# Row tiles for transposes and rotated scores, and a block transpose on DVE for a scan's input

## What is computed

```
# even layer: the scan's input, per group 512 + 128 + 128 channels
xbc = jax.nn.silu(causal_depthwise_conv(ssd_xbc, ssd_conv_w) + ssd_conv_b)
...
y_b = y_b.reshape(b_, l_, SSD_WIDTH) * jax.nn.silu(ssd_z.astype(jnp.float32))
# first block: 8 + 8 heads of 128, scores, softmax (or stick breaking), times v
z = jnp.einsum('bqhd,bkhd->bhqk', q[:, t0:t1], kb).astype(jnp.float32) * scale
# odd layer: 16 latent heads, 128 nope and 64 rotated channels
q_full = jnp.concatenate([q_nope, q_rope], axis=-1)
k_full = jnp.concatenate([k_nope, k_rope], axis=-1)
y_c = causal_block_attention(q_full, k_full, v) * jax.nn.silu(z_c)
```

## Time and profile before

| | |
|---|---|
| median of 3 runs (lowest, highest) | 2646.15 us (2645.53, 2647.1) |
| the profiled execution, its time | 2647.85 us |
| the profiled execution, its span | 2646.3 us |
| granted TensorE clock, mean | 0.999 |
| busy: PE / PE weight load / DVE / ACT / POOL | 2628.7 / 2181.9 / 1560.7 / 1346.5 / 337.9 us |

### The profile page before, as it was taken

The page is one execution under the profiler, slowest core; times in us unless marked ns, Lnnn a source line. Parts: engine busy times, 40 slices in busy tenths (PEclk is TensorE's granted clock), DMA queues, the critical chain, the costliest instruction groups (busy, mean ns, idle before and its releaser), DMA issues. The chain is left out here.

```text
span 2646.3 us, 35764 instructions
## 1 busy us (share of the span) xinstructions
PE 2628.7 (99%) x12125; PEld 2181.9 (82%) x12125; DVE 1560.7 (59%) x1825; ACT 1346.5 (51%) x1784; POOL 337.9 (13%) x523
## 2 busy tenths in 40 slices
PE   9999999999999999999999999999999999999998
PEld 7888888888878888888888888888888889888887
DVE  6444456667555555555555664445877855556864
ACT  6544455655444444444444654446665545554443
POOL 2100032211100000000000111000110010123400
PEclk9999999999999999999999999999999999999999
DMA  8966686678866767666666787666777777777864
GB/s 308 311 230 216 219 234 220 208 247 268 246 214 211 226 210 227 208 226 224 219 218 207 262 254 238 204 211 228 239 235 231 247 248 227 235 260 218 219 234 160
DMA packets 175722, 611.79 MB, mean 231 GB/s; under 512 B 23185, under 2 KB 26305, under 8 KB 175361
## 3 DMA queue, kind: packets, MB, share of 16 engines
q1 hardware_dynamic: 133632, 485.03, 55.4%
q0 software_dynamic: 37184, 121.07, 15.5%
q10 hardware_dynamic: 4800, 4.26, 0.6%
HBM read 559.36 MB, written 52.47 MB: 231 GB/s over the span
## 5 line engine op out<-in xcount | busy, mean ns | idle before, releaser
L1872 DVE TENSOR_TENSOR w_lo<-raw,w_hi 128x1024 fp32r<-128x1024 f32 x918 | 1115.4, 1222 | 850.9 <-ACT w_hi L1284 843.9
L1284 ACT ACTIVATE w_hi<-raw 128x1024 fp32r<-128x1024 f32 x919 | 963.8, 1058 | 901.0 <-PE acc L830 780.9
L824 PE MATMUL acc<-w_hi,x_t_hi 128*128 128x512 f32 (+1 forms) x2400 | 950.8, 396 | 0.4 <-ACT w_hi L1284 0.4
L824 PE MATMUL acc<-w_hi,x_t_lo 128*128 128x512 f32 (+1 forms) x2400 | 933.8, 389 | 0.0
L830 PE MATMUL acc<-w_lo,x_t_hi 128*128 128x512 f32 (+1 forms) x2400 | 640.0, 388 | 2.7 <-DVE w_lo L1872 2.7
L830 PEld LDWEIGHTS acc<-w_lo,x_t_hi 128*128 128x128 f32 x2400 | 450.5, 188 | 95.6 <-DVE w_lo L1872 3.1
L824 PEld LDWEIGHTS acc<-w_hi,x_t_hi 128*128 128x128 f32 x2400 | 451.4, 188 | 91.9 <-issue 1.9
L824 PEld LDWEIGHTS acc<-w_hi,x_t_lo 128*128 128x128 f32 x2400 | 451.4, 188 | 91.0 <-issue 1.9
L824 PE MATMUL acc<-w_hi,ff_t_hi 128*128 128x512 f32 x352 | 136.9, 389 | 0.0
L824 PE MATMUL acc<-w_hi,ff_t_lo 128*128 128x512 f32 x352 | 136.9, 389 | 0.0
L830 PE MATMUL acc<-w_lo,ff_t_hi 128*128 128x512 f32 x352 | 94.1, 389 | 0.0
(11 more groups left out here) (394 smaller groups left out, 2654.8 us busy)
## 6 DMA issues: line engine op xcount, KB each, us to landing
raw<-stream SPq DMA_DIRECT2D x919, 512.0 KB, 4.3
d_in<-tile POOLq DMA_DIRECT2D x20, 512.0 KB, 3.6
d_ev<-tile POOLq DMA_DIRECT2D x20, 512.0 KB, 4.9
d_x<-tile POOLq DMA_DIRECT2D x16, 512.0 KB, 4.2
r_b<-d_x POOLq DMA_DIRECT2D x64, 128.0 KB, 6.2
xin<-d_x POOLq DMA_DIRECT2D x16, 512.0 KB, 7.5
d_h<-tile POOLq DMA_DIRECT2D x14, 512.0 KB, 4.8
h_b<-d_h POOLq DMA_DIRECT2D x56, 128.0 KB, 4.5
```

What stands on the lines that cost most here:

```text
L824: nc.tensor.matmul(out, src[x][:, chunk + c, t * P:(t + 1) * P], w_hi[:, s, w], start=first and c == 0 and x == 0, stop=False)
L1284: nc.scalar.activation(w_hi[:, u.slot, :], raw[:, u.slot, :], ACT.Copy).then_inc(hi_ready, 1)
L1872: nc.vector.tensor_tensor(w_lo[:, s, :], raw[:, s, :], w_hi[:, s, :].bitcast(F32), ALU.subtract).then_inc(lo_ready, 1)
```

## The change

1. Scan: the 12 transposes of u are one block transpose on DVE (`turn_u`, after four loads of 32-partition blocks instead of three), with the weight's columns grouped for it; silu is ACT's own function instead of tanh and a product; the jobs of p = 9 to 14 move one unit later.
2. `turn_rows`: a transpose of 128 rows is written as two of 64 rows, at tile positions (0, 0) and (64, 0), into two banks. It takes the place of L1096 (8 blocks), L908 and L1234 (3 blocks each). The copies behind it are two instead of one. At L1234 the second bank is `ps_y[:, TOK:]`, with a wait on `l_y` at q = 3.
3. Latent scores: those of both heads of a pair stand at the even head's unit, nope in full matmuls, the rotated part as two row tiles of 64 rows, the heads in two banks, `ps_s` and `turn[0]`.
4. The loop of attention's four passes is written out on TensorE.

```
 HEAD_AT_UNIT = (1, 3, 6, 9)
+
+
+def rows_of(ap, h):
+    return ap.rearrange("p (b h n) -> p b h n", h=2, n=HALF)[:, :, h, :]
...
         def load_u(g):
-            pool.dma_start(u_in[:, :, 0:512], ev_v[:, :, bass.ds(g.times(512, 1024), 512)]).then_inc(s_u, 16)
-            for m in range(2):
-                pool.dma_start(u_in[:, :, 512 + m * P:640 + m * P],
-                               ev_v[:, :, bass.ds(g.times(P, 3072 + 512 * m), P)]).then_inc(s_u, 16)
+            for b in range(P // SQ):
+                w = 1024 + 768 * g.k + 6 * SQ * b
+                pool.dma_start(u_b[b * SQ:(b + 1) * SQ, :, :],
+                               d_ev[:, w:w + 6 * SQ].rearrange("(a j) n -> j a n", j=SQ)).then_inc(s_u, 16)
...
+        def turn_rows(blocks, banks=turn):
+
+            for n, src in enumerate(blocks):
+                for h in range(2):
+                    r = slice(HALF * h, HALF * (h + 1))
+                    mm = nc.tensor.transpose(banks[h][:, HALF * n:HALF * (n + 1)], src[r, :], ident[r, r],
+                                             tile_position=(HALF * h, 0))
+            return mm
+
         def turn_tile(n, src, ready, value):
 
             pe.wait_ge(ready, value)
@@ -904,10 +920,7 @@
                 if p == HEAD_AT_UNIT[j] + 5:
                     pe.wait_ge(at_prob[kind], m.times(1, 1))
                     pe.wait_ge(at_pt, J.times(1, 1))
-                    for c in range(3):
-                        mm = nc.tensor.transpose(turn[1][:, c * P:(c + 1) * P],
-                                                 prob[kind][:, c * P:(c + 1) * P], ident[:, :])
-                    mm.then_inc(at_pt_ps, 1)
+                    turn_rows([prob[kind][:, c * P:(c + 1) * P] for c in range(3)]).then_inc(at_pt_ps, 1)
...
-        with pe.Fori(0, 4) as i:
+        for i in range(4):
             for b in range(2):
                 pe.wait_ge(sums_out, blk("win", 12 + b, i).times(1, 1))
-            if p == 0:
-                pe.wait_ge(s_u, n.times(48, 48))
+            if p == 7:
                 pe.wait_ge(dt_v, 7)
                 pe.wait_ge(s_yb, n.times(1, 1))
-                for c in range(6):
-                    bank = (turn[0], turn[1], ps_s)[c // 2]
-                    for t in range(TH):
-                        mm = nc.tensor.transpose(bank[:, (c % 2 * TH + t) * P:(c % 2 * TH + t + 1) * P],
-                                                 u_in[:, t, c * P:(c + 1) * P], ident[:, :])
-                mm.then_inc(s_ut, 1)
-            if p == 7:
                 pe.wait_ge(s_silu, n.times(1, 1))
-                for t in range(TH):
-                    for c in range(4):
-                        mm = nc.tensor.transpose(turn[t][:, c * P:(c + 1) * P], cv[:, c, t * P:(t + 1) * P],
-                                                 ident[:, :])
-                mm.then_inc(s_xt, 1)
+                turn_rows([cv[:, c, t * P:(t + 1) * P] for t in range(TH) for c in range(4)]).then_inc(s_xt, 1)
                 nc.tensor.transpose(ps_s[:, 0:P], cv[:, 4, 0:P], ident[:, :])
                 for t in range(TH):
                     w = slice(t * P, (t + 1) * P)
                     mm = nc.tensor.matmul(ps_s[:, (1 + t) * P:(2 + t) * P], cv[:, 4, w], cv[:, 5, w],
                                           start=True, stop=True)
                 mm.then_inc(s_cb, 1)
-            if p == 9:
+            if p == 10:
                 pe.wait_ge(s_xde, n.times(1, 1))
                 nc.tensor.matmul(ps_s[:, :], bm_t[:, :], xde[:, :], start=True, stop=True).then_inc(s_st, 1)
-            if p == 11:
+            if p == 12:
                 pe.wait_ge(s_m, n.times(1, 1))
                 pe.wait_ge(s_xd, n.times(1, 1))
...
                     pe.wait_ge(l_qk, J // 2 + 1)
                     pe.wait_ge(l_qr, J // 2 + 1)
                     pe.wait_ge(l_z, J + 1)
-                    q_n, k_n, q_r = lqk[:, s, 0, :], lqk[:, s, 1, :], lr[J // 2 % 2]
-                    for out, qw, kw in ((ps_s[:, 0:P], slice(0, P), slice(0, P)),
-                                        (ps_s[:, P:H3], slice(P, TOK), slice(0, TOK))):
-                        nc.tensor.matmul(out, q_n[:, qw], k_n[:, kw], start=True, stop=False)
-                        mm = nc.tensor.matmul(out, q_r[:, qw], kr_t[:, s, kw], start=False, stop=True)
-                    mm.then_inc(l_scores, 1)
+                    q_r = lr[J // 2 % 2]
+                    parts = ((slice(0, P), slice(0, P), slice(0, P)), (slice(P, H3), slice(P, TOK), slice(0, TOK)))
+                    for at, qw, kw in parts:
+                        for e, bank in enumerate((ps_s, turn[0])):
+                            nc.tensor.matmul(bank[:, at], lqk[:, e, 0, qw], lqk[:, e, 1, kw], start=True, stop=False)
+                        for e, bank in enumerate((ps_s, turn[0])):
+                            r = slice(HALF * e, HALF * (e + 1))
+                            mm = nc.tensor.matmul(bank[:, at], q_r[r, qw], kr_t[r, e, kw], start=False, stop=True,
+                                                  tile_position=(HALF * e, 0))
+                    mm.then_inc(l_scores, 2)
                 if q == 3:
                     pe.wait_ge(l_exp, J + 1)
                     pe.wait_ge(l_qr, min((J + 1) // 2 + 1, 8))
-                    for c in range(3):
-                        mm = nc.tensor.transpose(turn[1][:, c * P:(c + 1) * P], lp[s][:, c * P:(c + 1) * P],
-                                                 ident[:, :])
-                    mm.then_inc(l_pt_ps, 1)
+                    pe.wait_ge(l_y, J + 1)
+                    turn_rows([lp[s][:, c * P:(c + 1) * P] for c in range(3)], (turn[1][:, :], ps_y[:, TOK:]))\
+                        .then_inc(l_pt_ps, 1)
                 if q == 4:
                     pe.wait_ge(l_pt, J + 3)
...
+            if p == 1 and g:
+                decays(n, 1)
             if p == 3 and g:
                 open_decays(n)
             if p == 4:
                 act.wait_ge(s_conv, n.times(3, 3))
-                nc.scalar.activation(th[:, :], cv[:, :, :].rearrange("p c t -> p (c t)"), ACT.Tanh)\
-                    .then_inc(s_th, 1)
-            if p == 5:
+                c_ = cv[:, :, :].rearrange("p c t -> p (c t)")
+                nc.scalar.activation(c_, c_, ACT.Silu, scale=2.0).then_inc(s_silu, 1)
                 act.wait_ge(s_z, n.times(16, 16))
-                nc.scalar.activation(zth[:, :, :], zt[:, :, :], ACT.Tanh, scale=0.5).then_inc(s_zth, 1)
+                nc.scalar.activation(zt[:, :, :], zt[:, :, :], ACT.Silu).then_inc(s_zs, 1)
             if p == 7:
                 act.wait_ge(s_xt, n.times(1, 1))
-                for t in range(TH):
-                    last = nc.scalar.activation(xs[:, t, :], turn[t][:, :], ACT.Copy)
+                for h in range(2):
+                    last = nc.scalar.activation(rows_of(xs[:, :, :].rearrange("p t n -> p (t n)"), h), turn[h][:, :],
+                                                ACT.Copy)
                 last.then_inc(s_xs, 1)
-            if p == 9:
+            if p == 10:
                 act.wait_ge(s_st, n.times(1, 1))
                 nc.scalar.activation(st[:, :], ps_s[:, :], ACT.Copy).then_inc(s_state, 1)
-            if p == 12:
+            if p == 13:
                 act.wait_ge(s_yg, n.times(1, 1))
                 for t in range(TH):
                     last = nc.scalar.activation(zth[:, t, :], yb[:, t, :], ACT.Square,
                                                 accum_out=g_ss[:, t:t + 1])
...
                     dve.wait_ge(at_pt_ps, J.times(1, 1))
-                    nc.vector.tensor_copy(p_t[s][:, :], turn[1][:, 0:H3]).then_inc(at_pt, 1)
+                    for h in range(2):
+                        last = nc.vector.tensor_copy(rows_of(p_t[s][:, :], h), turn[h][:, 0:H3 // 2])
+                    last.then_inc(at_pt, 1)
...
+        def turn_u(g):
+
+            dve.wait_ge(s_u, 64 * (g + 1))
+            dve.wait_ge(s_conv, 3 * g)
+            nc.vector.transpose(u_t[:, :, :].rearrange("p c (a i) -> p c a i", i=SQ),
+                                u_b[:, :, :].rearrange("p a (c i) -> p c a i", i=SQ)).then_inc(s_ut, 1)
...
-            if p == 5:
-                dve.wait_ge(s_th, n.times(1, 1))
-                c_ = cv[:, :, :].rearrange("p c t -> p (c t)")
-                nc.vector.scalar_tensor_tensor(out=c_, in0=th[:, :], scalar=1.0, in1=c_,
-                                               op0=ALU.add, op1=ALU.mult).then_inc(s_silu, 1)
-            if p == 6:
-                dve.wait_ge(s_zth, n.times(1, 1))
-                nc.vector.scalar_tensor_tensor(out=zt[:, :, :], in0=zth[:, :, :], scalar=1.0, in1=zt[:, :, :],
-                                               op0=ALU.add, op1=ALU.mult).then_inc(s_zs, 1)
...
+            if p == 10:
                 for t in range(TH):
                     x_ = xs[:, t, :].rearrange("p (h d) -> p h d", h=HG)
```

(50 more changed lines are left out.)

1 line of the change is left out of this document (removed).

## The result

| | before | changed |
|---|---|---|
| median (lowest, highest), 4 runs each | 2645.92 us (2645.53, 2647.1) | 2661.38 us (2658.57, 2664.95) |
| the profiled execution's span | 2646.3 us | 2660.8 us |
| granted TensorE clock, mean | 0.999 | 0.997 |

What follows compares the result with a forecast made beforehand. TensorE, busy 99% of the span, was taken to bound the kernel. Terms -5.3 - 1.1 + 5.5 - 0.3 + 0 + 9.5 = +8.3 on the median 2646.15 gave 2654.4, stated as 2654 us, range 2640 to 2664.

Steps and rivals of the forecast that it cites:

- The forecast's own narrower range: Whole kernel: the main forecast case, 2649 to 2660 us, chance 0.50.
- The new wait, +9.5: Latent transposes at odd heads: TensorE waits at q = 3 for DVE's eviction of `ps_y`, +9.5 us (0 to 11.4).
- The clock behind a stall: Latent stage, head 1: the granted clock can fall behind its wait, up to +1.7 us, left to the range.
- The scan, -6.7: Scan: u's transposes leave TensorE, -5.3 us; `xde` waits go, -1.1; cv as row tiles, -0.3; DVE's block transpose hidden.
- L1107's three waits: Scan: the weight load's three waits for `xde` go with jobs one unit later, -1.1 us (0 to -1.6).
- Table loads, 0: Scan, ACT: table loads at L1652 and L1628, 1.283 us each, hide before TensorE uses `w_hi`, costing nothing.
- A trip, 0.33: TensorE: switching to small tiles and back costs 0.33 us a round trip (bounds 0 and 0.4), paid 52 times.
- Three blocks as row tiles: Attention and latent heads: a three-block transpose costs 0.50 us instead of 0.33, +5.5 over 32.
- The pairs: Latent scores: two heads' rope parts side by side with two round trips cost 1.31 us as before, so 0.
- rival 1: All tile switches: free switches, without a drain; 52 round trips cost nothing, -2 to -9 us, about 2641; chance 0.14.
- the rival that they don't: Row-tile transposes, cv and rope: tiles run one after the other, 12.7 us more, 2665; chance 0.12.
- The rival of a hidden wait: Latent stage: DVE evicts in time, so the `l_y` wait is hidden; -1.2 us, 2645; chance 0.20.

Runs made afterwards that it cites:

- the first experiment: The kernel before with one line added, TensorE's wait for `l_y` at q = 3, transposes and scores unchanged: 2654.2 us, 1.0032 of before.

## Why the prediction was right, and where its sizes were off

The direction, the range and the main mechanism held: the changed kernel loses at the latent stage because TensorE waits there for `l_y`. The forecast's own narrower range did not: 2661.38 lies 1.4 above its 2660. And there was luck in the total, since the next terms erred in both directions.

1. **The new wait, +9.5.** The mechanism held: eight waits at the odd heads, none at the even ones, and the wait alone in the kernel before showed it once more. The size looks exact, but 9.5 is net of the 1.1 that head 1 waited for `lqk` before, and the list's 9.6 is not: net of it 8.5 are listed, and 8.7 are in the jobs. Head by head the margins were off by up to 1.3: 3.15 forecast and 1.87 measured at head 1, 2.06 and 1.40 at head 7, 0.32 and 0.64 at head 5. In the kernel before, where the margins were read, the same wait cost 7.5.
2. **The clock behind a stall, left to the range with at most 1.7.** Mis-sized: 4.6 in the profiled execution, at three stalls. It fell behind waits of 1.87 (head 1), 1.40 (head 3) and 1.39 (head 11), not only behind one as long as before's 2.71, and did not fall behind 1.40 (head 7) and 1.59 (head 15) of the same trace, nor in the latent stages of two kernels with waits of 2.25 and 1.7.
3. **The scan, -6.7.** This step failed. "I cost it at nothing" was said of the block transpose, since `w_lo` is made three units ahead. The lead was used up: DVE needs 3.5 us for a tap and a `w_lo` where TensorE needs 2.72, for three units. It needed that before as well, but its first tap started 1.41 ahead of unit 1's L830 (1836.32 and 1837.73), and in the changed kernel it starts 2.51 behind the same matmuls (1838.21 and 1835.70). Of these 3.9 us, 1.35 are TensorE's, which is there sooner without the transposes of u, and 1.35 go when the block transpose stands earlier (2.51 becomes 1.16); where the other 1.2 come from is not shown. TensorE pays 2.4 us for it at units 3 to 5: its L837 at 1838.42 and 1851.72 are four units apart, 13.30 where 10.88 is usual. Beside it, L1107's three waits went as forecast (-1.1), but group 0 has a new one for `xde` (+0.7); and the cv jobs of three groups, which now stand in the same gap as L1132, cost 1.1 more in all, 0.5 of it listed as waits for `z_t_lo`. Sum -2.5 by the jobs, -2.6 by the starts of the units.
4. **Table loads, 0.** The trace has no wait for `w_hi` on TensorE in the scan. Right.
5. **A trip, 0.33.** Measured 0.395 between two kernels that differ in it alone. Three blocks as row tiles: 0.50 forecast, 0.53 measured; 32 of them +6.0 and not +5.5. cv -0.09, as forecast, in the one group where the job stands alone. The pairs: 0 forecast, +1.0 measured. (In rival 1, 8.3 - 52 x 0.26 is -5.2 and not -5.3; nothing hangs on it.)
6. **Tiles overlap.** L865's halves start together; the rival that they don't is out. So is that of free switches. The rival of a hidden wait is out by the first experiment.

From the forecast's 8.3 to the 14.5 us of span: clock +4.6, scan +4.1, tiles and pairs +1.5, the wait -0.8, and before's own gap, which the changed kernel's trace hasn't, -3.6; with 0.2 elsewhere that makes 14.3. So 10.2 us of terms that were too small are seen as 6.2 because a gap that the edit does not touch and an overestimated wait ran the other way. The medians are 15.5 apart; the last 1.0 is within their interval.
